# Testing for spilled tokens ahead of the expert loop instead of behind it

## The reference

```python
g_sel = one_hot(argmax(h @ w_group_router))            # top-1 group of 4
top_v, top_i = top_k(expert logits inside the group, 2)  # top-2 of its 4 experts
top_w = softmax(top_v) * g_p
for gi in range(4):
    a = einsum('bsd,edf->bsef', h, w_e1[gi])
    b = einsum('bsd,edf->bsef', h, w_e3[gi])
    y = y + einsum('bsef,efd->bsd', silu(a) * b * w_all[:, :, gi, :, None], w_e2[gi])
x = x + g2 * y
```

## Time and profile before

| | |
|---|---|
| median of three runs | 2053.95 us |
| profiled execution, its own time | 2054.78 us |
| span of its instructions | 2053.0 us |
| PE busy | 1966.6 us (96%) |
| DVE, ACT, POOL busy | 698.5, 473.6, 98.6 us |
| chain that ended last | PE 86%, DMA 8%, others 6% |
| mean granted TensorE clock | 0.986 |
| expert loop of layer 0 | from 760.78 (first L1092) to 1036.71 (end of the last L1097) |
| expert loop of layer 1 | from 1739.31 to 2014.52 |

### The profile page before, as it was taken

The page is one execution under the profiler, slowest core; times in us unless marked ns, Lnnn a source line. Parts: engine busy times, 40 slices in busy tenths (PEclk is TensorE's granted clock), DMA queues, the critical chain, the costliest instruction groups (busy, mean ns, idle before and its releaser), DMA issues.

```text
span 2053.0 us, 29144 instructions
## 1 busy us (share of the span) xinstructions
PE 1966.6 (96%) x12526; PEld 1064.7 (52%) x12526; DVE 698.5 (34%) x1669; ACT 473.6 (23%) x926; POOL 98.6 (5%) x135
## 2 busy tenths in 40 slices
PE   6989999999999989999989999999999998999996
PEld 3444556656655544444445565665665554444443
DVE  1293366333311131222223956633331113122223
ACT  2301234344200131011133133334420002111112
POOL 0000100100000010000020010010000001000002
PEclk9999999999999989999999999999999999999998
DMA  9777671321222549999952223132213243999993
GB/s 400 250 292 271 218 261 46 111 108 62 89 96 102 205 159 349 390 393 393 396 205 110 86 89 128 46 106 96 79 62 123 103 202 147 349 391 391 390 399 124
DMA packets 45168, 421.67 MB, mean 205 GB/s; under 512 B 5888, under 2 KB 6032, under 8 KB 18928
## 3 DMA queue, kind: packets, MB, share of 16 engines
q1 hardware_dynamic: 30240, 369.43, 46.5%
q0 software_dynamic: 8080, 26.78, 3.8%
q10 hardware_dynamic: 6720, 23.60, 3.2%
HBM read 389.08 MB, written 28.61 MB: 203 GB/s over the span
## 4 chain that ended last, share of the span: by engine, by line
PE 86%; DMA 8%; ACT 1%; DVE 1%; another core or an unknown queue 1%; issue 1%; POOL 1%; SPq 0%; POOLq 0%; ACTq 0%; DVEq 0%
PE psum L988 16%; PE psum L734 16%; PE psum L1092 9%; PE psum L1003 8%; PE psum L737 6%; PE psum L1113 6%; DMA pc<-we_in 5%; PE psum L1097 5%; PE psum L1034 4%; DMA ring<-wmod_in 2%; PE psum L652 2%; PE psum L828 2%; DMA ring<-wch_in 1%; PE psum L712 1%; PE psum L1108 1%
## 5 line engine op out<-in xcount | busy, mean ns | idle before, releaser
L734 PE MATMUL psum<-hT,ring 128*128 128x384 f32 x1088 | 367.2, 491 | 2.0 <-ACT pc L1270 1.9
L988 PE MATMUL psum<-hT,ring 128*128 128x384 f32 x1024 | 343.2, 488 | 0.0
L734 PEld LDWEIGHTS psum<-hT,ring 128*128 128x128 f32 x1088 | 203.0, 191 | 145.6 <-issue 18.7
L988 PEld LDWEIGHTS psum<-hT,ring 128*128 128x128 f32 x1024 | 192.1, 190 | 130.6
L1003 PE MATMUL psum<-pc,ring 128*128 128x384 f32 x512 | 175.6, 486 | 0.0
L2119 DVE TENSOR_TENSOR ytok<-pc,psum 128x384 f32<-128x384 f32 x32 | 17.7, 554 | 342.7 <-ACT pc L1525 342.7
L2111 DVE COPY scr<-psum 64x512 f32<-64x512 f32 (+1 forms) x180 | 91.9, 510 | 114.8 <-PE psum L1113 113.2
L1003 PEld LDWEIGHTS psum<-pc,ring 128*128 128x128 f32 x512 | 95.4, 190 | 61.5
L1720 DVE SCALAR_TENSOR_TENSOR pc<-pc,par 128x384 f32<-128x384 f32 x240 | 127.2, 611 | 0.0
L737 PE MATMUL psum<-ring,hT 128*128 128x512 f32 x288 | 125.8, 594 | 0.0
L1937 DVE TENSOR_TENSOR mva<-mva,psum 128x384 f32<-128x384 f32 x48 | 26.6, 554 | 282.4 <-PE psum L1003 263.4
(11 more groups left out here) (338 smaller groups left out, 2022.0 us busy)
## 6 DMA issues: line engine op xcount, KB each, us to landing
ring<-we_in SPq DMA_DIRECT2D x48, 2048.0 KB, 18.5
pc<-we_in SPq DMA_DIRECT2D x48, 2048.0 KB, 18.9
ring<-wmod_in SPq DMA_DIRECT2D x42, 1024.0 KB, 5.9
ring<-wch_in SPq DMA_DIRECT2D x18, 2048.0 KB, 8.6
ring<-wgate_in SPq DMA_DIRECT2D x16, 2048.0 KB, 8.1
ring<-wbr_in SPq DMA_DIRECT2D x16, 1024.0 KB, 8.0
ring<-wtok_in SPq DMA_DIRECT2D x6, 2048.0 KB, 8.3
expert_out_rows<-scr ACTq DMA_DIRECT2D x30, 384.0 KB, 9.5
```

The source lines that it names most:

```text
L734: mm = pe.matmul(F[:, 0:T], wv[:, k, n * P:(n + 1) * P], hT[:, k, :], start=k == 0, stop=k == KD - 1)
L988: mm = pe.matmul(bank(5 + n % 2)[:, 0:T], wv[:, k, (n % 4) * P:(n % 4 + 1) * P], hT[:, k, :], start=k == 0, stop=k == KD - 1)
```

## The change

The test and the path behind it are moved on SP, PE, ACT and DVE from the end of the expert loop to a place ahead of it. The path's scratch `gu` moves from the first half of `scr` to the second, as the first half holds expert 0's tokens then; slot 3, in which the path loads its weights, is filled again at its end (one more DMA and one more wait, in the skipped path alone). ACT and DVE each get a further wait: ACT for `gu_ready` ahead of its first row load, DVE for `pick_ready` ahead of its read. Where the flag is 0, the same instructions are run as before.

```diff
-        gu = scr[:, 0:T]
+        gu = scrB[:, 0:T]
...
-        sp_w13 = sig("spill_input_weights_in", NF * 16)
+        sp_w13 = sig("spill_input_weights_in", (NF + 1) * 16)
...
@@ SP, behind the fills of experts 0 and 1 @@
                 fill(l, ("exp", 0, 1))
                 fill(l, ("exp", 1, 2))
+                sp.wait_ge(spill_known.sem, spill_known.at(l, 1))
+                spilled = sp.value_load(spill[0:1, 0:1], min_val=0, max_val=1)
+                with sp.If(spilled > 0):
+                    sp.wait_ge(slot_in[3].sem, SLOT[l, ("exp", 1, 0)][1])
...
+                    sp.dma_start(ring[3], block_of(l, ("exp", 1, 0))).then_inc(sp_w13.sem, 16)
+                with sp.Else():
+                    for s in (sp_w13, sp_w2):
+                        sp.sem_inc(s.sem, s.per_layer)
                 for e in range(NE - 1):
...
@@ PE @@
                 pe.wait_ge(ht_copied.sem, ht_copied.at(l, 7))
-                for e in range(NE - 1):
-                    hidden(e)
...
-                hidden(NE - 1)
                 pe.wait_ge(spill_known.sem, spill_known.at(l, 1))
                 spilled = pe.value_load(spill[0:1, 0:1], min_val=0, max_val=1)
                 with pe.If(spilled > 0):
-                    pe.wait_ge(xg_ready.sem, xg_ready.at(l, NE))
-                    pe.wait_ge(xy_ready.sem, xy_ready.at(l, 2 * (NE - 1)))
+                    pe.wait_ge(xh_ready.sem, xh_ready.at(l, 1))
...
+                    pe.wait_ge(sp_w13.sem, sp_w13.at(l, sp_w13.per_layer))
                 with pe.Else():
                     for s in (rtt_done, wb_done, ab_done, y_done):
                         pe.sem_inc(s.sem, s.per_layer)
+                for e in range(NE - 1):
+                    hidden(e)
...
+                hidden(NE - 1)
                 turn_hidden(NE - 1)
...
@@ ACT @@
                 ac.activation(last_pickT, bank(7)[:, 0:T], ACT.Copy).then_inc(ht_copied.sem, 1)
+                ac.wait_ge(spill_known.sem, spill_known.at(l, 1))
+                spilled = ac.value_load(spill[0:1, 0:1], min_val=0, max_val=1)
...
+                ac.wait_ge(gu_ready.sem, gu_ready.at(l, NF))
                 ac.wait_ge(scattered.sem, scattered.at(l, scattered.per_layer))
                 load_rows(1)
...
-                    if e == NE - 1:
-                        ac.wait_ge(spill_known.sem, spill_known.at(l, 1))
-                        spilled = ac.value_load(spill[0:1, 0:1], min_val=0, max_val=1)
...
@@ DVE @@
                 ve.wait_ge(spill_known.sem, spill_known.at(l, 1))
+                ve.wait_ge(pick_ready.sem, pick_ready.at(l, 2))
                 spilled = ve.value_load(spill[0:1, 0:1], min_val=0, max_val=1)
```

More of the change, by code:

```diff
@@ L596, in _ @@
                         fill(l, ("exp", NE - 1, 1))
-                sp.wait_ge(spill_known.sem, spill_known.at(l, 1))
-                spilled = sp.value_load(spill[0:1, 0:1], min_val=0, max_val=1)
-                with sp.If(spilled > 0):
-                    sp.wait_ge(xab_done.sem, xab_done.at(l, NE))
-                    with sp.Fori(0, NE) as i:
-                        for f in range(4):
-                            src = rearr(we13_d[bass.ds(l * 32 + i * 2 + f // 2, 1)]).rearrange("p (k n) -> p k n", k=KD)
-                            sp.wait_ge(ab_done.sem, l * NF + i * 4 + (f + 1))
-                            sp.dma_start(sp_w13_room, src[:, :, f % 2 * 256:f % 2 * 256 + 256]).then_inc(sp_w13.sem, 16)
-                            src = rearr(we2_d[bass.ds(l * 16 + i, 1)])
-                            sp.wait_ge(y_done.sem, l * NF * KD + i * 32 + (f * 8 + 1))
-                            sp.dma_start(sp_w2_room, src[:, f * D:(f + 1) * D]).then_inc(sp_w2.sem, 16)
-                    sp.wait_ge(y_done.sem, y_done.at(l, NF * KD))
-                with sp.Else():
-                    for s in (sp_w13, sp_w2):
-                        sp.sem_inc(s.sem, s.per_layer)
                 if l + 1 < DEPTH:
@@ L1178, in _ @@
                         pe.sem_inc(s.sem, s.per_layer)
+                for e in range(NE - 1):
+                    hidden(e)
+                    turn_rows(e + 1)
+                    if e >= 1:
+                        project(e - 1, 0)
+                        project(e - 1, 1)
+                    turn_hidden(e)
+                project(NE - 2, 0)
+                project(NE - 2, 1)
+                hidden(NE - 1)
                 turn_hidden(NE - 1)
@@ L1507, in _ @@
                 ac.activation(last_pickT, bank(7)[:, 0:T], ACT.Copy).then_inc(ht_copied.sem, 1)
+                ac.wait_ge(spill_known.sem, spill_known.at(l, 1))
+                spilled = ac.value_load(spill[0:1, 0:1], min_val=0, max_val=1)
+                with ac.If(spilled > 0):
+                    with ac.Fori(0, NF) as i:
+                        ac.wait_ge(wb_done.sem, l * NF + i + 1)
+                        ac.activation(wb, bank(6)[:, 0:T], ACT.Copy).then_inc(wb_ready.sem, 1)
+                        ac.wait_ge(ab_done.sem, l * NF + i + 2)
+                        ac.activation(e_t[:, 0, :], bank(0)[:, 0:T], ACT.Silu).then_inc(a_exp.sem, 1)
+                with ac.Else():
+                    for s in (wb_ready, a_exp):
+                        ac.sem_inc(s.sem, s.per_layer)
                 def load_rows(e):
@@ L1529, in _ @@
                         load_rows(e + 3)
-                    if e == NE - 1:
-                        ac.wait_ge(spill_known.sem, spill_known.at(l, 1))
-                        spilled = ac.value_load(spill[0:1, 0:1], min_val=0, max_val=1)
-                        with ac.If(spilled > 0):
-                            with ac.Fori(0, NF) as i:
-                                ac.wait_ge(wb_done.sem, l * NF + i + 1)
-                                ac.activation(wb, bank(6)[:, 0:T], ACT.Copy).then_inc(wb_ready.sem, 1)
-                                ac.wait_ge(ab_done.sem, l * NF + i + 2)
-                                ac.activation(e_t[:, 0, :], bank(0)[:, 0:T], ACT.Silu).then_inc(a_exp.sem, 1)
-                        with ac.Else():
-                            for s in (wb_ready, a_exp):
-                                ac.sem_inc(s.sem, s.per_layer)
                     ac.wait_ge(xgt_done.sem, xgt_done.at(l, e + 1))
@@ L2161, in _, with open_hidden @@
                 ve.wait_ge(y_used.sem, y_used.at(l, NF * KD))
+                def open_hidden(e):
+                    ve.wait_ge(xs_ready.sem, xs_ready.at(l, e + 1))
+                    if e >= 1:
+                        ve.wait_ge(xgt_done.sem, xgt_done.at(l, e))
+                    ve.tensor_tensor(x_g, x_s, x_ab[:, :, 1, :], ALU.mult).then_inc(xg_ready.sem, 1)
+                for e in range(NE - 1):
+                    open_hidden(e)
+                    if e >= 1:
+                        keep_out(e - 1)
+                keep_out(NE - 2)
+                open_hidden(NE - 1)
                 for t in range(NT):
```

27 lines of the change are left out of this document (9 added, 18 removed).

## The result

The changed kernel takes 2064.4 us (median of five, 2063.16 to 2069.69) beside 2051.02 us for the kernel before (median of five): ratio 1.0064, 95% interval 1.0051 to 1.0077. It is slower by 13.4 us. The profiled execution took 2067.03 us (span 2065.2).

What follows compares the result with a forecast made beforehand. PE bounds the kernel (86% of the chain). Terms +3.6 + 2.5 - 0.5 = +5.6 us on the profiled 2054.78 give 2060.4, or 2059.5 from the median of 2053.95; range 2046.5 to 2063.5.

Steps and rivals of the forecast that it cites:

- The front's test, 2 x 1.8 = +3.6: Ahead of expert 0, PE's moved read, branch, increments and two weight waits lie on the path, 1.8 us a layer: +3.6.
- that only the test comes on top of the front's stand: Ahead of expert 0, ACT's copy, already 1.5 us late in layer 0 beside POOL's indirect DMA, gets no later: 0.
- Clock at the fronts, +2.5: At expert 0's first matmuls (L1092), both layers, PE's longer stand lowers its granted clock: +2.5 us, bounds 0 and +5.3.
- Rear batch, -0.5: At the loop's end, the last hidden batch (L1097) gets shorter without the register read beside it: -0.5 us, bounds -1.0 and 0.
- Rear wait stays, 0: Behind the last hidden batch, the SiLU's 3.4 us wait, laid to POOL's gather, stays: 0, with -11.2 as bound.
- its two front terms, 6.1 in all: Ahead of expert 0 in both layers: the test on PE's path, +3.6 us, and the lost clock, +2.5 us.
- The second case: Between L1097 and L1525 of expert 15, the rear wait belonged to the test and goes: net -5.1, 2048.8 us; chance 0.30.
- The third: The stall is the branch's and moves with it to the fronts: +3.5 us, 2057.5; chance 0.12.
- the 4 us named as the sign: Ahead of expert 0, a gap of 4 us or more between ACT's copy (L1507) and L1092 would show the third.
- The fourth: The front test hides because spill is read early, the rear keeps its wait: within 1 us of before; chance 0.08.

Runs made afterwards that it cites:

- the prompt chip: Kernel before and changed kernel, both unaltered, timed again on a chip showing no late semaphores: 2045.55 us beside 2039.79, ratio 1.0028.
- the wait moved: Changed kernel with PE's wait for ACT's copies put behind the test: 2037.66 us, ratio 0.9995; on a chip with late semaphores 2061.77, ratio 1.0012.
- late gather: Kernel before with POOL's gather held until DVE has the last expert's product: 2049.73 us; on a chip with late semaphores 2063.73.
- PE's test alone in front: Kernel before with only PE's test and skipped path moved ahead of the expert loop, run twice: 2048.17 us, ratio 1.0040; 2049.41, ratio 1.0051.
- the read alone: Kernel before without any test or slow path, plus only PE's read of the flag ahead of the expert loop: 2046.29 us, ratio 1.0027.

## Why the prediction was wrong

- **Where the time came out.** The forecast of 2059.5 us was 4.9 below the median, but it was reckoned from 2053.95; beside the 2051.02 of the comparison its +5.6 stands against +13.4. The terms of its sum follow.
- **The front's test, 2 x 1.8 = +3.6: mis-sized.** Measured from the copy's end to the first matmul, less the 0.05 us that stood there before, it was 2.05 + 2.43 = 4.5 us in the first comparison, and 2.27 + 2.38 = 4.65 more of stand on the prompt chip. The durations were taken from the rear, beside a gather; in front, beside the scatter, the read took 0.55 and 0.92 us instead of 0.49 and 0.31. That it lies bare because it waits for the same `ht_copied` was right, and shown from the other side by the wait moved.
- **The step that failed: that only the test comes on top of the front's stand.** The prediction saw ACT's copy 1.5 us late at the front of the earlier trace rows, gave it to POOL, and took it as a constant. It grew: from the transposes' end (758.71, 1738.27) to the second copy's end (760.73, 1739.26) were 2.02 and 1.0 us before, and 3.06 and 3.81 after, +3.9 us. This 0 in my sum is the largest single miss.
- **Clock at the fronts, +2.5: measured** 1.23 + 1.75 = +3.0 (L1094 10.01 and 8.84 against 8.78 and 7.09), and 1.69 + 1.56 = +3.25 on the prompt chip. The second front did not keep its clock.
- **Rear batch, -0.5: measured** 3.81 and 4.30 against 4.06 and 4.27, -0.2. It was not the read that held the last matmul: with the read and a late gather it takes 3.66.
- **Rear wait stays, 0: right**, with the right owner: 4.05 and 3.40 us instead of 3.4 and 3.4. PE's stands there grew by 0.6 in all and L1110 shrank by 0.4.
- **The sum.** 4.5 + 3.9 + 3.0 - 0.2 + 0.6 - 0.4 = 11.4, against 12.25 between the two profiled executions and 13.4 between the medians. Without late semaphores 4.65 + 3.25 = 7.9, against a measured +5.8 (interval +2.4 to +9.2). That the forecast of +5.6 is near this is luck: it was made for a chip that holds semaphores, and its two front terms, 6.1 in all, stand for 7.9 even here.
- **The rivals.** The second case (the rear wait goes) is refuted by the changed kernel itself and by the late gather. Its best evidence, two unexplained SiLUs of 32 and a test behind each, was a coincidence of place: the gather stands there too. The third (the jump's stall moves along) is refuted: four increments run behind the jump at 51 ns each, the first matmul is 2.10 and 2.48 us behind the copy instead of the 4 us named as the sign, and with the wait moved the whole test is free. The fourth did not come.
- Lengths of single instructions held: the compare-and-branch took 335 and 377 ns in front, again far from the about 108 ns of the Trainium skill (Advanced Engine Details and Errata, Control Flow Timing).

## What to carry to other kernels

In this kernel a test of 1 to 2 us on PE left it standing 0.24 us at most behind a batch, nothing ahead of a wait, and cost its full length behind a wait: put the test first and the wait behind it, which here made the moved test free (2037.66 against 2045.55 us, each beside a kernel before of 2039.4 and 2039.8). Take the length of a register read from the place where it will stand. And where a wait is put down to nothing that the profile knows, delay the DMA suspected beside it on the same chip before believing in the instruction that happens to be next, and do not carry a hold over as a constant: here the one in front grew by 3.9 us when the tests moved, for a reason still open.

## What the runs showed of the hardware

- The same kernel differs from chip to chip (or from occasion to occasion, which these runs do not part). The kernel before took 2039.2 to 2039.9 us on four chips, 2058.5 on a fifth and 2051 in the first comparison; only in the last two was ACT released late by PE beside POOL's indirect DMAs. Between the first profile (2054.78) and a prompt one (2039.89) lie 14.9 us, and the edges of the loop account for it: stands 1.12 + 0.09 in front and 3.33 + 3.36 at the rear, the last batches 0.40 + 0.61, L1092 of layer 0 1.69, L1108 2.97 + 2.01, together 15.6.
- A register read of a flag in SBUF took 0.28 to 0.55 us away from the scatter and 0.46 to 1.08 beside or just behind it, on four engines; PE's reads 2.5 us behind the scatter's last DMA took 0.35 and 0.49 again. The Trainium skill (DMA: Bandwidth & Descriptors, Latency and other measured facts) has a floor of about 600 ns for a `tensor_load`; the traces have it at less than half of that, down to 275 ns for this flag.
- The granted clock is not a function of the last stand alone. In the traces of prompt chips the same stands of 1.20 us and 0.63 us were followed by 7.08 us of L1108 in 19 layers of 28 and by 8.77 or 8.78 in nine: both layers of three traces (the two of PE's test alone in front, and the read alone) and one layer of three others. In front, stands of 3.19 and 2.96 us were followed by 8.78 and 7.09 us of L1092 in one and the same trace. With the read alone, stretches at the rear of layer 0 (columns as in the earlier trace rows) read

```profile
1036.00:1038.00 2.00, 0.55 (x3) 0.31 (x3) 0.55 (x1) 0.74 (x2) 1.39 (x3) 1.00 0.90 338
1038.00:1040.00 2.00, 1.66 (x3) 0.81 (x4) 0.33 (x1) 1.39 (x2) 0.89 (x1) 0.70 1.03 313
1040.00:1042.00 2.00, 2.00 (x3) 0.57 (x2) 0.95 (x1) 0.37 (x1) 0.00 (x0) 0.50 0.92 342
```

where the prompt kernel before keeps 1.00. What decides it was not found; it is worth 1.7 us a time, so a local sum of this kernel is not better than a few us.
